# Modulation weights by feature halves, an earlier second slab, and its split beside VectorE's products

## What is computed

```python
mod = c @ w_ada + b_ada                     # c: 1 x 1024, w_ada: 1024 x 6144
sh1, sc1, gt1, sh2, sc2, gt2 = split(mod, 6)
h = rms_norm(x, g_pre_mix) * (1 + sc1) + sh1
proj = h @ w_in                             # 1024 x 5120
```

## Time and profile before

| | before |
|---|---|
| median of 3 runs | 1486.69 us (1484.39 to 1486.77) |
| profiled execution | 1484.37 us |
| its span, first to last instruction | 1482.6 us |
| TensorE busy | 1440.1 us (97%) |
| VectorE, ScalarE, GpSimd busy | 851.4, 552.9, 990.2 us |
| mean DMA rate over the span | 113 GB/s |
| first 1/40 of the span (37 us): TensorE busy, DMA rate | 3 tenths, 349 GB/s |

### The profile page before, as it was taken

The page is one execution under the profiler, slowest core; times in us unless marked ns, Lnnn a source line. Parts: engine busy times, 40 slices in busy tenths (PEclk is TensorE's granted clock), DMA queues, the critical chain, the costliest instruction groups (busy, mean ns, idle before and its releaser), DMA issues.

```text
span 1482.6 us, 18612 instructions
## 1 busy us (share of the span) xinstructions
PE 1440.1 (97%) x6987; PEld 1169.7 (79%) x6987; DVE 851.4 (57%) x1334; ACT 552.9 (37%) x1075; POOL 990.2 (67%) x400
## 2 busy tenths in 40 slices
PE   3999999999999999999999999999999999999997
PEld 3888877778898888888898844789789888888886
DVE  6998156554565555666744786441516555465655
ACT  3201133433454344444333376452424523333214
POOL 1857554355668899888568996365153989788653
PEclk9999999999999999999999999999999999999999
DMA  9875321223543332322443200133024323232131
GB/s 349 298 270 209 100 85 57 86 86 106 169 153 114 114 113 87 114 86 85 156 126 109 86 1 1 59 125 123 7 86 142 114 86 114 86 114 86 57 97 74
DMA packets 103385, 167.88 MB, mean 113 GB/s; under 512 B 3917, under 2 KB 61185, under 8 KB 102785
## 3 DMA queue, kind: packets, MB, share of 16 engines
q1 hardware_dynamic: 100176, 160.45, 31.7%
q10 hardware_dynamic: 3121, 6.26, 1.4%
HBM read 161.97 MB, written 4.72 MB: 112 GB/s over the span
## 4 chain that ended last, share of the span: by engine, by line
PE 84%; DVE 10%; ACT 3%; DMA 2%; issue 1%; POOL 1%; DVEq 0%; SPq 0%; ACTq 0%; POOLq 0%
PE bank L911 25%; PE bank L913 25%; PE bank L912 25%; DVE bank L2054 2%; DMA ada_w<-in_w_ada 1%; DVE smx L2507 1%; DVE x L2050 1%; PE bank L1372 1%; PE bank L1429 1%; PE bank L1448 1%; DVE bank L2050 1%; PE bank L1183 1%; DVE m L2050 1%; ACT junk L1541 1%; PE bank L1195 1%
## 5 line engine op out<-in xcount | busy, mean ns | idle before, releaser
L911 PE MATMUL bank<-ht_hi,w_hi 128*128 128x512 f32 (+1 forms) x1200 | 442.9, 369 | 0.5 <-DVE ht_lo L2050 0.3
L912 PE MATMUL bank<-ht_hi,w_lo 128*128 128x512 f32 (+1 forms) x1200 | 440.1, 367 | 0.0
L913 PE MATMUL bank<-ht_lo,w_hi 128*128 128x512 f32 (+1 forms) x1200 | 440.0, 367 | 0.0
L759 POOL TENSOR_TENSOR w_lo<-w_raw,w_hi 128x2048 fp32r<-128x2048 f32 x83 | 389.8, 4697 | 6.9
L757 POOL TENSOR_SCALAR w_hi<-w_raw 128x2048 fp32r<-128x2048 f32 x83 | 162.3, 1955 | 343.5 <-DMA w_raw<-in_w_in 111.2
L911 PEld LDWEIGHTS bank<-ht_hi,w_hi 128*128 128x128 f32 x1200 | 226.5, 189 | 41.6 <-issue 2.7
L913 PEld LDWEIGHTS bank<-ht_lo,w_hi 128*128 128x128 f32 x1200 | 226.6, 189 | 37.1
L912 PEld LDWEIGHTS bank<-ht_hi,w_lo 128*128 128x128 f32 x1200 | 226.6, 189 | 36.8 <-issue 0.5
L809 POOL TENSOR_TENSOR dn_lo<-dn_raw,dn_hi_all 128x1024 fp32r<-128x1024 f32 x77 | 184.6, 2418 | 56.7 <-ACT dn_hi_all L1738 56.6
L2054 DVE SCALAR_TENSOR_TENSOR uc<-bank,par,uc 128x511 f32<-128x511 f32 x88 | 66.0, 750 | 128.7 <-ACT uc L1992 125.6
L823 POOL TENSOR_TENSOR dn_raw<-dn_raw 128x1024 f32<-128x1024 f32 x44 | 105.8, 2404 | 12.8 <-PE bank L913 4.8
(11 more groups left out here) (305 smaller groups left out, 2415.7 us busy)
## 6 DMA issues: line engine op xcount, KB each, us to landing
w_raw<-in_w_in SPq DMA_DIRECT2D x27, 1024.0 KB, 5.0
ada_w<-in_w_ada SPq DMA_DIRECT2D x48, 512.0 KB, 7.3
w_raw<-in_w_up SPq DMA_DIRECT2D x22, 1024.0 KB, 5.0
w_raw<-in_w_mlp_in SPq DMA_DIRECT2D x16, 1024.0 KB, 5.5
dn_raw<-in_w_mlp_out SPq DMA_DIRECT2D x28, 512.0 KB, 4.8
w_raw<-in_w_out SPq DMA_DIRECT2D x8, 1024.0 KB, 5.0
w_raw<-in_w_mem_kv SPq DMA_DIRECT2D x8, 1024.0 KB, 5.2
dn_raw<-in_w_down SPq DMA_DIRECT2D x16, 512.0 KB, 4.7
```

The lines of the kernel that those rows point to most:

```text
L759: g.tensor_tensor(w_lo[:, r], w_raw[:, r], w_hi[:, r].bitcast(F32), ALU.subtract).then_inc(slab_split, 1)
L911: inc_free(pe.matmul(o, ah, bh, start=start, stop=False))
L912: pe.matmul(o, al, bh, start=False, stop=False)
L913: return pe.matmul(o, ah, bl, start=False, stop=stop)
```

## The change

- Modulation tiles 0 to 15 hold something else: tiles 0 to 7 are the shift and scale weights (columns 0 to 511 and 1024 to 1535) of features 0 to 511, tiles 8 to 15 those of features 512 to 1023. `first_sums(s)` therefore makes both for one half of the features, in one PSUM tile of its own. Each partition's 4 KB come as two rows of 2 KB.
- SyncE loads slab 0 ahead of tile 0, the blocks of x behind tiles 0, 1, 2 and 3, and slab 1 ahead of tile 14 instead of behind product 15. Slab 2 follows tile 15 without a wait.
- VectorE inverts the roots behind products 1, 2, 3 and 4, and copies the vectors behind product 5. `first_mod(0)` stands behind product 9. Then it alternates: product 10, low part of chunk 0, product 11, chunk 1, product 12, chunk 2, product 13, chunk 3, products 14 and 15, `first_mod(1)`, and the other four chunks as before.
- ScalarE scales and shifts chunks 0 to 3, all four, makes their high parts, and then the high part of slab 1 (a copy of 128 by 2048). Chunks 4 to 7 stay shared with VectorE.
- GpSimd splits slab 0 as soon as it has landed. Of slab 1 it makes only the low part, when ScalarE's high part is there.
- TensorE turns all blocks (six chunks), makes the first sums and starts with slab 0. Chunk 6 is turned in stage 1, ahead of its triples; the second sums stand in stage 3 behind three of its seven triples, and chunk 7 is turned ahead of the last one.

```diff
--- before.py
+++ after.py
@@ -43,9 +43,9 @@
 POOL_PAIRS = 2
 LOW_TAPS = 4
 ADA_BUFS = 7
-X_WITH = (5, 7, 9, 11)
-NORM_WITH = (7, 9, 11, 13)
-VEC_WITH = 11
+X_WITH = (0, 1, 2, 3)
+NORM_WITH = (1, 2, 3, 4)
+VEC_WITH = 5
 POOL_TAPS = (2, 2, 3)
 TAPS_BEFORE_ROPE = (2, 2, 2, 2, 12)
 TAPS_BEHIND_K = 16
@@ -453,7 +453,7 @@
         psum_free = [sem(f"psum_free{b}") for b in range(BANKS)]
         slab_loaded = [sem(f"slab_loaded{r}") for r in range(RING)]
         slab_hi, slab_split, slab_free = sem("slab_hi"), sem("slab_split"), sem("slab_free")
-        slab_go, first_lo = sem("slab_go"), sem("first_lo")
+        slab_go, first_lo, second_hi = sem("slab_go"), sem("first_lo"), sem("second_hi")
         c_loaded, rows_loaded, mem_loaded = sem("c_loaded"), sem("rows_loaded"), sem("mem_loaded")
         x_loaded = [sem(f"x_loaded{m}") for m in range(NT)]
         ada_b_loaded = [sem(f"ada_b_loaded{i}") for i in range(2)]
@@ -599,19 +599,25 @@
                 if i >= ADA_BUFS:
                     sp.wait_ge(ada_used, i - ADA_BUFS + 1)
                 s = i // DC
-                sp.dma_start(ada_w[:, r], wada[:, i % DC, s * D:(s + 1) * D]).then_inc(ada_loaded[r], 16)
-
+                if s < 2:
+                    sp.dma_start(ada_w[:, r].rearrange("p (j n) -> p j n", j=2),
+                                 wada[:, i % DC, 0:2 * D].rearrange("p (j n) -> p j n", j=2)[:, :, 512 * s:512 * s + 512]
+                                 ).then_inc(ada_loaded[r], 16)
+                else:
+                    sp.dma_start(ada_w[:, r], wada[:, i % DC, s * D:(s + 1) * D]).then_inc(ada_loaded[r], 16)
+
+            win = w_rows(A["w_in"])
+            load(raw4, win[:, 0:4, 512:1024])
             for i in range(2 * DC):
+                if i == 2 * DC - 2:
+                    load(raw4, win[:, 4:8, 512:1024])
                 ada(i)
                 if i in X_WITH:
                     m = X_WITH.index(i)
                     sp.dma_start(x[:, m], A["x"][m * P:m * P + P, :]).then_inc(x_loaded[m], 16)
-            win = w_rows(A["w_in"])
             i = 2 * DC
             for c0 in (512, 1024, 0, 1536, 2048, 2560):
-                for s in range(2):
-                    if n == 1:
-                        sp.wait_ge(ada_used, 2 * DC)
+                for s in range(0 if c0 != 512 else 2, 2):
                     load(raw4, win[:, 4 * s:4 * s + 4, c0:c0 + 512])
                     for _ in range(4 if n > 2 else 0):
                         if i < 6 * DC:
@@ -755,13 +761,12 @@
                 g.wait_ge(slab_loaded[r], i * 16 + 16 * (n // RING + 1))
                 g.sem_inc(slab_go, 1)
                 g.tensor_scalar(w_hi[:, r], w_raw[:, r], 1.0, 1.0, ALU.mult, ALU.mult).then_inc(slab_hi, 1)
-                g.wait_ge(slab_hi, i * RING + n + 1 - (FF1_J - 2 if n >= S0["memkv2"] - 2 else 0))
+                g.wait_ge(slab_hi, i * RING + n - (FF1_J - 2 if n >= S0["memkv2"] - 2 else 0))
                 g.tensor_tensor(w_lo[:, r], w_raw[:, r], w_hi[:, r].bitcast(F32), ALU.subtract).then_inc(slab_split, 1)
 
             def split_first():
 
                 g.wait_ge(slab_loaded[0], 16)
-                g.wait_ge(ada_used, 2 * DC)
                 g.tensor_scalar(w_hi[:, 0], w_raw[:, 0], 1.0, 1.0, ALU.mult, ALU.mult).then_inc(slab_hi, 1)
                 g.wait_ge(slab_hi, 1)
                 raw, hi, lo = (w[:, 0].rearrange("p (k n) -> p k n", k=4) for w in (w_raw, w_hi, w_lo))
@@ -800,7 +805,8 @@
             taps = conv31()
             n = S0["w_in2"] + 6
             split_first()
-            split(1)
+            g.wait_ge(second_hi, 1)
+            g.tensor_tensor(w_lo[:, 1], w_raw[:, 1], w_hi[:, 1].bitcast(F32), ALU.subtract).then_inc(slab_split, 1)
             split_all(2, S0["mlp"])
 
             def split_down(u, w):
@@ -919,7 +925,8 @@
                 for t in ts:
                     Tile(t).wait_taken(pe)
 
-            def features(t0, ks, ah, al, i=None, tper=0, sper=0, n=T, each=None, first=False, behind=None):
+            def features(t0, ks, ah, al, i=None, tper=0, sper=0, n=T, each=None, first=False, behind=None,
+                         within={}):
 
 
                 for s in range(ks):
@@ -936,7 +943,9 @@
                             each(new)
                             Tile(t0 + new).wait_free(pe)
                             pe.wait_ge(first_lo if new < 3 else slab_split, new + 1 if new < 3 else 1)
-                            for m, k in [(m, new) for m in range(new)] + [(new, k) for k in range(new + 1)]:
+                            for at, (m, k) in enumerate([(m, new) for m in range(new)] + [(new, k) for k in range(new + 1)]):
+                                if (new, at) in within:
+                                    within[new, at]()
                                 c = slice(m * P, m * P + P)
                                 mm3(Tile(t0 + m).ap[:, 0:n], wh[:, k, c], wl[:, k, c], ah[:, k], al[:, k], k == 0, False)
                         state["owed"] += 1
@@ -1106,13 +1115,13 @@
 
                 pe.wait_ge(ada_used, DC * (s + 1))
                 for c in range(DC):
-                    t = Tile(T0["ada01"] + c // 4)
-                    if s == 0 and c % 4 == 0:
+                    t = Tile(T0["ada01"] + s)
+                    if c == 0:
                         t.wait_free(pe)
-                    at = DC * s + c
+                    at = DC * (c // 4) + 4 * s + c % 4
                     ins = pe.matmul(t.ap[:, at:at + 1], ada_acc[:, s, c * P:c * P + P], ones[:, 0:1], start=True,
                                     stop=True)
-                    if s == 1 and c % 4 == 3:
+                    if c == DC - 1:
                         ins.then_inc(t.full, 1)
 
             def modulation(s):
@@ -1143,14 +1152,16 @@
             for m in range(NT):
                 if m == 1:
                     turn_rows()
-                if m == NT - 1:
-                    first_sums(0)
                 first_rows(range(DC - 2), m)
-            first_sums(1)
-            for c in (DC - 2, DC - 1):
+            first_sums(0)
+
+            def first_chunk(c):
                 for m in range(NT):
                     first_rows((c,), m)
-            features(T0["w_in"], 2, ht_hi, ht_lo, each=lambda k: Tile(NT1_T[k]).wait_taken(pe), first=True)
+
+            features(T0["w_in"], 2, ht_hi, ht_lo, each=lambda k: Tile(NT1_T[k]).wait_taken(pe), first=True,
+                     within={(1, 0): lambda: first_chunk(DC - 2), (3, 3): lambda: first_sums(1),
+                             (3, 6): lambda: first_chunk(DC - 1)})
             for c in range(1, 5):
                 features(T0["w_in"] + 4 * c, 2, ht_hi, ht_lo)
             tokens(T0["w_in"] + 20, 2, ht_hi, ht_lo)
@@ -1641,14 +1652,25 @@
                 norm_stat("nt1", m, x[:, m])
                 act.wait_ge(norm_inv, NB["nt1"] + m + 1)
                 st.done(act.activation(xn1[:, m], x[:, m], ACT.Copy, scale=stat[:, 16 + m:17 + m]), xn_ready)
-            for pair in range(DC // 2):
+            def first_affine(c):
+                t = Tile(NT1_T[c])
+                t.wait_full(act)
+                st.done(act.activation(t.ap[:], t.ap[:], ACT.Identity, scale=mod[:, 1, c:c + 1], bias=mod[:, 0, c:c + 1]))
+
+            Tile(T0["ada01"]).wait_taken(act)
+            for c in range(4):
+                first_affine(c)
+                act.wait_ge(act_step, st.value(act_step))
+                st.done(act.copy(ht_hi[:, c], Tile(NT1_T[c]).ap[:]), nt1_hi)
+            act.wait_ge(slab_loaded[1], 16)
+            st.done(act.copy(w_hi[:, 1], w_raw[:, 1]), second_hi)
+            for pair in range(DC // 4, DC // 2):
                 c = 2 * pair + 1
                 if pair % 2 == 0:
                     Tile(T0["ada01"] + pair // 2).wait_taken(act)
                 t = Tile(NT1_T[c])
-                t.wait_full(act)
-                st.done(act.activation(t.ap[:], t.ap[:], ACT.Identity, scale=mod[:, 1, c:c + 1], bias=mod[:, 0, c:c + 1]))
-                act.wait_ge(nt1_affine, pair + 1)
+                first_affine(c)
+                act.wait_ge(nt1_affine, pair - DC // 4 + 1)
                 st.done(act.copy(ht_hi[:, c - 1], Tile(NT1_T[c - 1]).ap[:]), nt1_hi)
                 act.wait_ge(act_step, st.value(act_step))
                 st.done(act.copy(ht_hi[:, c], t.ap[:]), nt1_hi)
@@ -2172,7 +2194,7 @@
                         if j % 2:
                             stt(mod[:, j], mod[:, j], 1.0, col((V_G1, V_GM1)[j // 2], 8), ALU.add, ALU.mult)
 
-            for i in range(2 * DC):
+            for i in range(DC):
                 ada_product(i)
                 if i in NORM_WITH:
                     norm_inv_of("nt1", NORM_WITH.index(i))
@@ -2201,13 +2223,17 @@
                 v.wait_ge(nt1_hi, c + 1)
                 tt(ht_lo[:, c], t.ap[:], ht_hi[:, c].bitcast(F32), ALU.subtract, tile=t)
 
+            for i in range(DC, DC + 2):
+                ada_product(i)
             first_mod(0)
-            first_affine(0)
```

(11 more changed lines are left out.)

## The result

| | before | changed kernel |
|---|---|---|
| median | 1486.42 us (9 runs, 1484.08 to 1488.25) | 1491.28 us (9 runs, 1489.67 to 1498.51) |
| ratio to before | | 1.0042, 95% interval 1.0031 to 1.0053 |
| profiled execution, its span | 1484.37, 1482.6 us | 1489.79, 1488.1 us |

The change makes the kernel slower: by 4.9 us if the medians are compared, by 6.2 (4.6 to 7.9) if the ratio is; the forecast was 1489.9, 3.2 above before. First the timeline of the changed kernel, all engines in one list. Its lines are numbered anew: L2076 and L2081 are the modulation products, L2072 the low parts and small operations of VectorE, L2083 its scaling of chunks 4 and 6, L763, L765 and L809 GpSimd's conversion and subtractions, L1122 the sums, L917 to L919 the triples.

The account below looks back on a forecast made before the run. After the prologue TensorE was taken to bound the kernel. Slab 1's second tile starting 2.4 us later, plus 0.8 for the clock and 0 afterwards, gave 3.2 on the median 1486.69: 1489.9 us, range 1486.2 to 1494.5.

Parts of the forecast that it names:

- first sums: TensorE's sums of the first eight modulation tiles, held by VectorE's norms and products: 26.9 to 30.3 us, against 28.3 before.
- M: Start of VectorE's last small operation of the first modulation half, from which later prologue times are counted: 30.75 us.
- first product: TensorE's first product in the prologue: M + 2.4 = 33.1 us instead of 37.8.
- collision: In the prologue, VectorE's products 14 and 15 wait for GpSimd's splits; product 15 ends at 47.35 us, undisturbed M + 11.8.
- the stop: TensorE stands still ahead of its second sums, waiting for product 15: 2.3 us, until 47.4.
- rival 1: The collision doesn't happen or matter: second tile at 53.1, +0.2 us, time 1486.9, not slower; chance 22.
- second tile: TensorE's start of slab 1's second output tile, where the change is read: 55.3 us against 52.89, +2.4.
- the turn: In the prologue, VectorE's product 13 starts 0.4 us ahead of GpSimd's request for slab 1's low part, so goes first.
- Rival 2: GpSimd goes ahead of product 13: product 15 ends at 52.3 us, TensorE stops 6 us, +9.0, 1495.7; chance 12.
- the chain behind the second sums: Second sums, VectorE's small operations, last chunks and slab 1's start, up to the second tile: 47.4 to 55.3 us.
- the clock behind the new stop: TensorE's granted clock falls after its stop ahead of the second sums: 0.8 us put in, bounds 0 and 1.7.
- Afterwards: Behind the prologue, VectorE's lag vanishes and SyncE's queue and GpSimd shift with TensorE: added cost 0, bound 1 us.

Follow-up runs that it names:

- E1: Changed kernel with GpSimd's low part of slab 1 held back until VectorE's product 15 is done: 1487.89 us, ratio 1.0023.
- E2: Changed kernel with only GpSimd's split of slab 2 held back until product 15 is done: 1489.41 us, ratio 1.0031.
- E4: Changed kernel with the edits of E1 and E3 together: 1486.74 us, ratio 1.0009.
- E3: Changed kernel with ScalarE's three loads (bias row, two gains) issued directly behind its copy of slab 1's high part: 1490.24 us, ratio 1.0034.
- E7: The kernel before, unchanged, profiled again for a second trace: 1486.82 us.
- E6: E5 with the low parts of chunks 1 to 3 each a product earlier on VectorE: 1484.76 us, ratio 0.9992.
- E8: The kernel before with slab 0 loaded ahead of tile 0 and split at once: 1486.59 us, ratio 1.0010.
- E5: E4 with VectorE's vector copy and scale behind product 9 and row 3's inverse behind product 5: 1484.89 us, ratio 0.9995.

## Why the prediction came out as it did

**Right: where it loses, and by what.** The first sums at 26.9 were 26.42, M at 30.75 was 30.43, the first product at 33.1 was 32.88. The collision was forecast as 4.7 and 2.75 us for products 14 and 15 and measured as 4.65 and 2.73; product 15 ended at 46.92 against 47.35, and the stop was 2.19 against 2.3. E1, E2 and E4 show that this collision is the cause and not only beside it: without it 2.8 (E1) to 3.7 us (E4 against E3) come back by the ratios, and without half of it the stop shrinks to 0.2. The Trainium skill (SBUF — State Buffer, "SBUF: two separate sides") calls the port pair that the two engines share an exclusive lock: of a VectorE instruction with two SBUF inputs and a GpSimd one that reads SBUF, whichever starts first holds it for the whole instruction. The traces agree: product 14 takes 4.65 us beside GpSimd, and 14 and 15 take 2.67 together in E1 without it.

**Right: rival 1's arithmetic.** With no collision it gave a second tile at 53.1, +0.2, and nothing won. E4 is that case, with the later wait removed too: 53.72, and a ratio of 1.0009.

**Right, narrowly: the turn.** Rival 2 hung on product 13 being 0.4 us ahead of GpSimd's request. It was 0.44 ahead, and the turn fell as forecast; half a microsecond the other way was priced at +9.0 and stays untried.

**Too short: the chain behind the second sums.** From the start of the sums to the second tile the forecast has 7.9 us (47.4 to 55.3); E1, where the clock stays up, has 8.76 (44.83 to 53.59). Of the 0.9 missing, 0.54 is a pause of VectorE between its last small operation and its first scaling (the row at 50.16; in E1 at 47.81), for which the sum has no term. Product 15's being 0.4 early takes half of it back.

**Too small: the clock behind the new stop.** The term was 0.8 (bounds 0 and 1.7). The changed kernel's second tile is 3.22 behind E1's, of which 2.19 is the stop: about 1.0 is left for the clock. E3's is 1.67 more. So 1.0 in one trace, near 2.7 in the other, the second beyond the bound.

**Wrong: "Afterwards. Added cost: 0, bound 1".** The step that failed is the sentence that SyncE's queue and GpSimd "follow the release of the slabs, so they shift with TensorE". VectorE did catch up (its fourth product of the next group ends at 60.98, forecast 61.2), but the step counted only queues that shift, and not what they now meet: the three loads at the end of ScalarE's part of the norm, which the change moved next to slab 3's. Between the second tile and slab 8 the distance grows from 73.44 (before) to 74.77, 1.3 us, beyond the bound of 1. E3 shows the loads to be the reason: with them moved, the distance is 73.45 again. The prediction named tiles and slabs, and forgot the DMAs of the engine whose work it had moved.

**Placed now:** the 2.3 us between before's profiled execution and its median, for which the prediction had no row. E7's trace, a time of that group, has them in the clock at three places. The forecast summed on the first trace; against the second, the second tile is +3.15 and the profiled time +2.97.

Together, in the traces: the second tile is 3.9 late (2.4 and 0.8 forecast), slab 8 another 1.3 (0 forecast), the rest is 0.2, so 5.4 where 3.2 was forecast. By the ratios, each with the one before it taken off: collision, stop and its clock 2.8 (E1), the loads 2.1 (E4), and what is left between E4 and before, 1.3 (-0.6 to 3.3), make 6.2. So the forecast had the way and the main term right and the size at half to two thirds; that 1489.9 is only 1.4 off the median is helped a little by its starting from 1486.69, which is 0.3 above what before's median became. Still open are why E6's earlier second tile didn't shorten the median, and where E8's later one was given back.

## What to carry to other kernels

Before work is moved to a second engine, lay its instructions in time against those of VectorE with two SBUF operands: here a wait that delays GpSimd's subtraction by 4.6 us makes the kernel about 3 us faster (2.8 in E1, 3.7 in E4 against E3, by the ratios), because the products it would block are what TensorE waits for. When a block of an engine's work moves, write down the loads that stand at its end, too, and what they will share the queues with. And where clock falls move single executions by 2 us, take a second trace of the unchanged kernel before explaining such a difference.

## What the runs showed of the hardware

- **The same stop does not always bring the clock down.** TensorE waits 3.2 or 3.3 us for VectorE at one place of the program in all ten traces, whatever the kernel; the wait ends between 227 (before) and 236 us (E1). In four of them (before, E1, E3, E5) the mean granted clock of the window from 226 to 240 us is 0.88, in the other six it is 1.00. Elsewhere the clock fell behind stops of 2.2 (changed kernel, 47 us; E1, 129 us) and 2.9 us (E3), and did not behind 1.1 (changed kernel, slab 8) and 1.7 us (E2, slab 8).
- **The clock also falls without any stop, behind sums with one column.** Behind the 32 passes that start between 170 and 177 us TensorE is busy all the time, and yet in nine of ten traces the clock is low there for 3.4 or 6.8 us (means of 0.91 and 0.83 from 170 to 190 us). The prediction took from the tenth, the only one it had, that such sums don't lower it. No run here took the sums away, so that they are the cause isn't shown.
- **Three broadcast loads of half a megabyte each stretch the 1 MB load beside them** from 5.0 (before, and E3, where they are issued earlier) to 8.7 us (changed kernel).
